# Weighted latent sums of sparse attention: 4-byte products replaced by three rounded ones

## Chip, cores and metric

The kernel runs on one core of a Trainium2 chip. The metric is the device time of one execution in microseconds (us); the median of a few runs is compared. The engines are TensorE (PE: matmuls, and transposes, which are matmuls against the identity), VectorE (DVE), ScalarE (ACT), GpSimd (POOL), and SyncE (SP), which issues the transfers. Each runs its own list of instructions in order, and they wait for each other by semaphores.

## What is computed

One decoder layer over 528 tokens (16 learned meta tokens and 512 others) of width 1024: a half-weighted SwiGLU layer, a mixer, a second SwiGLU layer, each followed by a residual sum and a layer norm. The change lies in the mixer's attention group (8 heads). An indexer scores every causal key, the 128 best of each query are kept, and all heads attend over one shared latent of 128 numbers per token:

```python
s = jnp.einsum('bqhc,bqkc->bqhk', q_lat, kv_sel) * (ATT_HEAD_DIM ** -0.5)
p = jax.nn.softmax(s, axis=-1)
o_lat = jnp.einsum('bqhk,bqkc->bqhc', p, kv_sel)          # the weighted latent sums
y_att = jnp.einsum('bthc,hcd->bthd', o_lat, w_uv)
```

The kernel keeps all keys and adds -1e30 to the scores of those not picked. The other head group, an mLSTM of 4 heads, is interleaved with attention.

## The kernel before

Tokens are cut into five tiles: tile 0 is the 16 meta tokens, tiles 1 to 4 have 128 tokens each. Most products are split products: ScalarE rounds a 4-byte operand to fp32r (`hi`), VectorE or GpSimd subtracts that from the operand (`lo`), and hi·hi + hi·lo + lo·hi is summed in PSUM (`split_product`). Each of the three is one TensorE instruction in the trace. Attention's products are plain 4-byte ones, and each is two instructions in the trace.

Attention works in 8 groups G of four heads: query tile j = 1 + G//2, heads 4·(G%2) to 4·(G%2)+3. Every engine has a loop over G = 0 to 8 written out by hand, and in step G it handles the scores of group G and the weighted sums of group G-1:

- **TensorE** (line 1733): `scores` (four, into two pairs of PSUM banks, so that score k waits for the masking of score k-2), `turn` (line 1696: transposes the four heads' exponentials of one key tile i into PSUM bank t%2, four instructions), `weigh` (line 1709: the latents of key tile i times the turned exponentials of four heads, 512 columns, summed over the key tiles 0 to j in bank 3). `project` (line 1717) and `turn_y` (line 1726) follow after every second group, and `turn_mlstm` brings in the other head group. For the last group, before the projections begin, there are five key tiles.
- **VectorE** (line 2377): `masked` (line 2331: score plus mask from PSUM into SBUF, with the row maximum, then its negative into nmax), `copy_even` (line 2363: turned exponentials of even t from PSUM to SBUF, which `weigh` reads), `normalise`, `att_lo` (the remainder of the attention output), the last rounds of the selection of tile 4 (`late_round`: maximum and replace, 8 keys each), `normed_mlstm` and `gated_mlstm` for the other heads.
- **ScalarE** (line 1098): `exps` (one exponential per head, with its row sum), `copy_odd` (line 1087), the copy of the finished sums into `olt`, `att_hi`, `mlstm_hi`, and one weight rounding (`hi`, line 725).

There are 28 turns and 28 weighs in all: 2, 2, 3, 3, 4, 4, 5, 5. In the order of before, step G of TensorE has the first two `scores`, `project` (of the pair finished in the step before), `turn` of tiles 0 and 1, the other two `scores`, then for each tile i the `turn` of tile i+1 (from the third on) followed by `weigh` of tile i, and at the end `turn_mlstm` and `turn_y`. On VectorE follow each other `masked` of the first two heads, `normalise`, `copy_even` of tiles 0 and 1, a late round, in step 2 the norm of the last mLSTM head (`normed_mlstm`), `masked` of the other two heads, the mLSTM gating, `copy_even` of the other tiles, `att_lo`, a late round.

Ahead of attention stand the mixer's projections (units 0 to 9), whose weights are rounded by ScalarE's `hi` and whose remainders are made by VectorE (`lo`) or GpSimd (`mix_lo`, line 627), and VectorE's selection (`select`, line 2194) and convolution (`convolve`, line 2231). GpSimd's list also has the causal masks (`causal_mask`, line 663), of which the last lets the `masked` of tile 4 begin.

## Time and profile before

| what | us |
|---|---|
| median of three runs (1017.17 to 1018.02) | 1017.67 |
| the profiled execution, its own time | 1017.49 |
| the span of its instructions | 1015.8 |
| around the span | 1.69 |

The profile is one execution, recorded by the hardware. Busy time is per engine; the end of a matmul is modelled, so a busy TensorE is not one at its peak. The chain of work is followed back from the last instruction, each step to what released it. In the chain a piece of TensorE is counted from completion to completion, so a row of it gives what an instruction adds when others stand next to it. The granted clock of TensorE was 1.00 of the higher of its two levels (2.4 GHz) in all the stretches shown below.

### The profile page before, as it was taken

The numbers are of one execution on the slowest core, as the hardware profiler recorded it, in microseconds if no ns is written. First come the engines' busy times: TensorE is split into PE (matmuls) and PEld (weight loads), VectorE is DVE, ScalarE is ACT, GpSimd is POOL, SyncE is SP. The second block draws the span as 40 slices with busy tenths as digits, with TensorE's granted clock in tenths as the row PEclk, the third lists the DMA queues.
The fourth block names the chain that finished last, engine by engine and source line by source line (L and its number), as shares of the span: only waits on it lengthen the run. The fifth ranks groups of instructions, "written<-read, shape, count | busy, mean of one in ns | idle before, by whom it ended". The sixth has DMA issues, their size and how long they took to land.

```text
span 1015.8 us, 18999 instructions
## 1 busy us (share of the span) xinstructions
PE 996.9 (98%) x7028; PEld 907.9 (89%) x7028; DVE 714.0 (70%) x1317; ACT 493.8 (49%) x868; POOL 118.1 (12%) x92
## 2 busy tenths in 40 slices
PE   9999999999999999999999999999999999999996
PEld 8999999999999988699765668889999999988886
DVE  6988888887322264699997523699989889942236
ACT  6656665566121264546346522576656665812121
POOL 0000000001121262045302205320000000000000
PEclk9999999999999999999999999999999999999999
DMA  7233332323223313132110102113323232333212
GB/s 252 84 100 107 102 105 90 116 80 105 86 86 111 113 44 116 36 123 82 44 42 1 43 1 83 43 42 126 124 83 124 85 121 96 125 103 101 98 57 84
DMA packets 30849, 90.48 MB, mean 89 GB/s; under 512 B 4689, under 2 KB 5329, under 8 KB 30801
## 3 DMA queue, kind: packets, MB, share of 16 engines
q1 hardware_dynamic: 30800, 89.83, 26.7%
q8 instruction: 31, 0.51, 0.2%
q14 instruction: 18, 0.14, 0.0%
HBM read 87.72 MB, written 2.10 MB: 88 GB/s over the span
## 4 chain that ended last, share of the span: by engine, by line
PE 81%; DVE 15%; ACT 2%; issue 1%; DMA 0%; SPq 0%; DVEq 0%; ACTq 0%
PE ps L1229 38%; PE ps L1287 22%; PE ps L1152 9%; DVE sc L2201 3%; DVE top L2200 3%; PE ps L1714 2%; PE ps L1424 1%; PE ps L1692 1%; DVE qk L2240 1%; PE ps L1705 1%; DVE wlo L1877 1%; PE ps L1489 1%; PE ps L1722 1%; PE ps L1337 1%; PE ps L1335 1%
## 5 line engine op out<-in xcount | busy, mean ns | idle before, releaser
L1229 PE MATMUL ps<-tsum,whi 128*128 128x264 f32 (+1 forms) x1280 | 243.1, 282 | 0.5 <-ACT ht L790 0.5
L1229 PEld LDWEIGHTS ps<-tsum,whi 128*128 128x128 f32 x1280 | 202.3, 188 | 0.7 <-issue 0.7
L1229 PE MATMUL ps<-tsum,wlo 128*128 128x264 f32 (+1 forms) x640 | 180.3, 282 | 0.0
L1229 PE MATMUL ps<-xh,whi 128*128 128x264 f32 (+1 forms) x480 | 135.4, 282 | 0.3 <-ACT sil L790 0.3
L1229 PE MATMUL ps<-xl,whi 128*128 128x264 f32 (+1 forms) x480 | 135.5, 282 | 0.0
L1229 PE MATMUL ps<-xh,wlo 128*128 128x264 f32 (+1 forms) x480 | 135.3, 282 | 0.0
L729 ACT ACTIVATE whi<-wraw 128x1408 fp32r<-128x1408 f32 (+1 forms) x48 | 74.6, 1555 | 123.0 <-PE ps L1287 123.0
L1787 DVE TENSOR_TENSOR wlo<-wraw,whi 128x1408 fp32r<-128x1408 f32 (+1 forms) x38 | 70.0, 1843 | 85.3 <-ACT whi L729 85.3
L1287 PE MATMUL ps<-hh,whi 128*128 128x264 f32 (+1 forms) x462 | 124.2, 323 | 0.0
L1287 PE MATMUL ps<-hh,wlo 128*128 128x264 f32 (+1 forms) x462 | 123.5, 322 | 0.0
L1287 PE MATMUL ps<-hl,whi 128*128 128x264 f32 (+1 forms) x462 | 123.4, 321 | 0.0
L777 ACT ACTIVATE whi<-ws 128x512 fp32r<-128x512 f32 x160 | 100.2, 628 | 42.5 <-PE ps L1229 40.5
L1229 PEld LDWEIGHTS ps<-tsum,wlo 128*128 128x128 f32 x640 | 120.2, 188 | 0.0
L1877 DVE TENSOR_TENSOR wlo<-ws,whi 128x512 fp32r<-128x512 f32 x160 | 109.5, 685 | 9.8 <-ACT whi L777 7.8
L1877 DVE TENSOR_TENSOR wlo<-wraw,whi 128x512 fp32r<-128x512 f32 x120 | 82.2, 686 | 26.2 <-ACT whi L777 26.2
L1152 PE MATMUL ps<-xh,whi 128*128 128x512 f32 (+1 forms) x296 | 96.2, 360 | 2.3 <-ACT xh L925 2.0
L1152 PE MATMUL ps<-xh,wlo 128*128 128x512 f32 (+1 forms) x296 | 92.6, 348 | 0.0
L1229 PEld LDWEIGHTS ps<-xl,whi 128*128 128x128 f32 x480 | 90.6, 189 | 0.0
L1229 PEld LDWEIGHTS ps<-xh,whi 128*128 128x128 f32 x480 | 90.1, 188 | 0.5 <-issue 0.5
L1229 PEld LDWEIGHTS ps<-xh,wlo 128*128 128x128 f32 x480 | 90.1, 188 | 0.0
L1152 PE MATMUL ps<-xl,whi 128*128 128x512 f32 (+1 forms) x296 | 88.0, 347 | 0.0
L777 ACT ACTIVATE whi<-wraw 128x512 fp32r<-128x512 f32 x120 | 74.7, 627 | 19.6 <-PE ps L1229 17.3
(287 smaller groups left out, 1828.0 us busy)
## 6 DMA issues: line engine op xcount, KB each, us to landing
wraw<-in_ffn_w_gate SPq DMA_DIRECT2D x43, 512.0 KB, 4.2
wraw<-in_ffn_w_up SPq DMA_DIRECT2D x42, 512.0 KB, 4.3
wraw<-in_ffn_w_down SPq DMA_DIRECT2D x32, 384.0 KB, 3.2
wraw<-in_ffn_w_down SPq DMA_DIRECT2D x32, 320.0 KB, 3.5
wraw<-in_w_in SPq DMA_DIRECT2D x19, 512.0 KB, 4.5
wraw<-in_w_out SPq DMA_DIRECT2D x8, 512.0 KB, 4.4
out<-zrow SPq DMA_DIRECT2D x8, 256.0 KB, 2.0
x<-in_x SPq DMA_DIRECT2D x3, 528.0 KB, 7.5
```

What stands on the lines that cost most here:

```text
L729: act.activation(whi[:, s, 0:width], wraw[:, s, 0:width], ACT.Copy).then_inc(w_hi, 1)
L777: act.activation(block_of(whi, b), block_source(g, b), ACT.Copy).then_inc(*done)
L1152: mm = pe.matmul(ps[:, b + e, 0:width], w, mov, start=(first and n == 0), stop=(last and n == 2))
L1229: mm = pe.matmul(ps[:, bank, 0:(HT, HALF_SEQ)[p // 2]], w[:, k * P:(k + 1) * P], v[:, k, :], start=(first and k == 0 and n == 0), stop=(k ...
L1287: mm = pe.matmul(ps[:, b + e, 0:width], w, mov, start=(kk == 0 and n == 0), stop=(kk == FT - 1 and n == 2))
L1335: pe.matmul(dst, w_h, a_h, start=(kk == 0), stop=False)
L1337: mm = pe.matmul(dst, w_h, a_l, start=False, stop=(kk == FT - 1))
L1714: pe.matmul(ps[:, 3, :], cmat[0:ROWS[i], i, :], pt_flat[0:ROWS[i], (t % 2) * 512:(t % 2 + 1) * 512], start=(i == 0), stop=(i == 1 + G // 2 ...
L1787: dve.tensor_tensor(wlo[:, s, 0:width], wraw[:, s, 0:width], whi[:, s, 0:width].bitcast(F32), ALU.subtract)\
L1877: dve.tensor_tensor(block_of(wlo, b), block_source(g, b), block_of(whi, b).bitcast(F32), ALU.subtract)\
L2200: link(dve.max(top8[:, r % 2, :], w))
L2201: link(dve.match_replace(w, top8[:, r % 2, :], w, TAKEN))
```

## The change

Each weigh becomes a split product. The latents are split once: ScalarE rounds them (`chi`, 128x640, on its list between the copies of `ct` and the rounding of unit 4's weights), GpSimd subtracts in place (`clo`) and builds `meta_c`, the rounded meta latents twice in 64 rows (`split_latents`, between `mix_lo(9)` and `causal_mask(3)`). Every turned tile is rounded by ScalarE (`weights_hi`) and its remainder is taken by VectorE (`weights_lo`), one after the other, in place of one copy by either; the three products are chi·hi, clo·hi and chi·lo. For the meta tile 32 rows are turned in place of 16, the remainder goes to rows 32 to 63 beside the rounded part, and two products do: clo on 16 rows and `meta_c` on 64.

The order of the three loops changes too. On ScalarE the roundings of tiles 0 and 1 stand ahead of the group's exponentials, those of tiles 2 to 4 between them. On VectorE the remainders of tiles 0 to 2 stand ahead of the third `masked`, that of tile 3 ahead of the fourth, that of tile 4 behind it; `normalise`, `att_lo`, the mLSTM work and the late rounds all stand behind the fourth `masked`. On TensorE `turn_y` moves one step later, behind the first two turns, and `project` also stands behind those turns. Two rounds of the late selection stand in step 4 and one in step 5, as before, but at the end of these steps.

```diff
-HEAD_GATED = ((1, 0), (1, 1), (2, 1), (3, 1))
-HEAD_HI = ((1, 1), (2, 0), (3, 0), (4, 0))
+HEAD_GATED = (1, 1, 2, 3)
+HEAD_HI = (2, 2, 3, 4)
-LATE_AT = ((4, 0), (4, 1), (5, 0))
+LATE_AT = (4, 4, 5)
...
+            c_parts = sb("c_parts", [P, NT, 256], F32R, s)
+            clo, chi = c_parts[:, :, 0:LAT], c_parts[:, :, LAT:2 * LAT]
...
+            pts = sb("pts", [P, NT * ML_H * VW], F32R, s)
+            meta_c = sb("meta_c", [64, LAT], F32R, s)
...
+        pt_h = [pts[:, e * 512:(e + 1) * 512] for e in range(2)]
+        pt_l = [pts[:, (2 + e) * 512:(3 + e) * 512] for e in range(2)]
...
+                def split_latents():
+                    pool.wait_ge(c_hi, 1)
+                    pool.wait_ge(ct_turned, 1)
+                    pool.tensor_tensor(clo, cmat, chi.bitcast(F32), ALU.subtract).then_inc(c_lo, 1)
+                    m = N_META
+                    link(pool.memset(meta_c[:, :].bitcast(F32), 0.0))
+                    for e, r in enumerate((0, 32)):
+                        pool.wait_ge(c_lo, e + 1)
+                        pool.tensor_copy(meta_c[r:r + m, :], chi[0:m, 0, :].bitcast(F32)).then_inc(c_lo, 1)
+                    pool.wait_ge(c_lo, 3)
...
                 mix_lo(9)
+                split_latents()
                 causal_mask(3)
...
                 act.activation(ct[:, END[3]:T], ps[:, 5, 0:P], ACT.Copy).then_inc(ct_ready, 1)
+                act.activation(chi[:, :, :], cmat, ACT.Copy).then_inc(c_hi, 1)
                 hi(MIX0 + 4, 0, UW, False)
...
+                def weights_hi(G, tiles):
                     for i in tiles:
                         t = TP0[G] + i
...
+                        R = META_ROWS if i == 0 else P
+                        act.wait_ge(pt_turned, t + 1)
+                        if t >= 2:
+                            act.wait_ge(pv_step, t - 1)
+                        act.activation(pt_h[t % 2][0:R, :], ps[0:R, t % 2, :], ACT.Copy).then_inc(pt_hi, 1)
+                late, turned_late = None, None
                 for G in range(GROUPS + 1):
...
+                    last_tile = 1 + (G - 1) // 2
+                    if G >= 1:
+                        weights_hi(G - 1, (0, 1))
+                    for q in range(4):
                         if G < GROUPS:
...
+                            exps(G, (q,))
+                        if G >= 1 and 2 + q <= last_tile:
+                            weights_hi(G - 1, (2 + q,))
+                    if turned_late is not None:
+                        att_hi(turned_late)
+                    turned_late = None
                     if G >= 1:
                         j, g = 1 + (G - 1) // 2, (G - 1) % 2
...
                         act.wait_ge(pv_step, TP0[G])
                         if G - 1 >= 2:
                             act.wait_ge(y_done, j - 1)
                         act.activation(olt[g], ps[:, 3, :], ACT.Copy).then_inc(ol_ready, 1)
+                        for h in range(ML_H):
+                            if HEAD_HI[h] == G:
+                                mlstm_hi(h)
                         if G == 4:
                             hi(MIX0 + 11, 1, UW, True)
...
+                        turned_late, late = late, j if g == 1 else None
...
+                        pe.wait_ge(pt_lo, t - 1)
                     for q in range(4):
...
+                        k0, k1 = (START[i], END[i]) if i else (0, META_ROWS)
+                        mm = pe.transpose(ps[0:k1 - k0, t % 2, q * P:(q + 1) * P], pbuf[G % 2][:, q, k0:k1], ident[:, :])
                     mm.then_inc(pt_turned, 1)
                 def weigh(G, i):
                     t = TP0[G] + i
...
+                    if i == 0:
+                        pe.wait_ge(pt_hi, t + 1)
+                        if G >= 1:
+                            pe.wait_ge(ol_ready, G)
+                        pe.wait_ge(c_lo, 3)
+                        m = N_META
+                        pe.matmul(ps[:, 3, :], clo[0:m, 0, :], pt_h[t % 2][0:m, :], start=True, stop=False)
+                        pe.wait_ge(pt_lo, t + 1)
+                        pe.matmul(ps[:, 3, :], meta_c[:, :], pt_h[t % 2][0:64, :], start=False, stop=False).then_inc(pv_step, 1)
+                        return
+                    pe.wait_ge(pt_hi, t + 1)
+                    pe.matmul(ps[:, 3, :], chi[:, i, :], pt_h[t % 2], start=False, stop=False)
+                    pe.matmul(ps[:, 3, :], clo[:, i, :], pt_h[t % 2], start=False, stop=False)
+                    pe.wait_ge(pt_lo, t + 1)
+                    pe.matmul(ps[:, 3, :], chi[:, i, :], pt_l[t % 2], start=False, stop=(i == 1 + G // 2)).then_inc(pv_step, 1)
...
+                late, turned_late = None, None
                 for G in range(GROUPS + 1):
                     last_tile = 1 + (G - 1) // 2
...
+                    if G < GROUPS:
+                        scores(4 * G)
+                        scores(4 * G + 1)
+                    if G == 0:
+                        turn_mlstm((0, 1))
                     if G >= 1:
...
+                        turn(G - 1, 0)
+                        turn(G - 1, 1)
+                    if late is not None:
+                        project(late)
+                    if turned_late is not None:
+                        turn_y(turned_late)
+                    if G < GROUPS:
+                        scores(4 * G + 2)
+                    if G >= 1:
+                        weigh(G - 1, 0)
+                        if last_tile >= 2:
+                            turn(G - 1, 2)
+                            weigh(G - 1, 1)
+                        if last_tile >= 3:
+                            turn(G - 1, 3)
+                    if G < GROUPS:
+                        scores(4 * G + 3)
+                    if G >= 1:
+                        for i in range(1 if last_tile < 2 else 2, last_tile + 1):
                             weigh(G - 1, i)
+                            if 4 <= i + 2 <= last_tile:
+                                turn(G - 1, i + 2)
                         if G in (1, 2):
                             turn_mlstm((G + 1,))
...
+                        turned_late, late = late, last_tile if (G - 1) % 2 else None
...
+                def weights_lo(G, tiles):
                     for i in tiles:
                         t = TP0[G] + i
...
+                        dve.wait_ge(pt_hi, t + 1)
+                        if i == 0:
+                            ins = dve.tensor_tensor(pt_h[t % 2][32:32 + META_ROWS, :], ps[0:META_ROWS, t % 2, :],
+                                                    pt_h[t % 2][0:META_ROWS, :].bitcast(F32), ALU.subtract)
+                        else:
+                            ins = dve.tensor_tensor(pt_l[t % 2], ps[:, t % 2, :], pt_h[t % 2].bitcast(F32), ALU.subtract)
+                        ins.then_inc(pt_lo, 1)
+                def late_rounds(G):
+                    for n, at in enumerate(LATE_AT):
+                        if at == G:
+                            select(4, LATE_ROUND + n, LATE_ROUND + n + 1)
+                turned_late = None
                 for G in range(GROUPS + 1):
                     last_tile = 1 + (G - 1) // 2
...
+                    if G < GROUPS:
+                        masked(4 * G)
+                        masked(4 * G + 1)
                     if G >= 1:
...
+                        weights_lo(G - 1, range(min(last_tile, 2) + 1))
+                    if G < GROUPS:
+                        masked(4 * G + 2)
+                    if G >= 1 and last_tile >= 3:
+                        weights_lo(G - 1, (3,))
+                    if G < GROUPS:
+                        masked(4 * G + 3)
+                    if G >= 1 and last_tile >= 4:
+                        weights_lo(G - 1, (4,))
+                    if late is not None:
+                        normalise(late)
+                    if turned_late is not None:
+                        att_lo(turned_late)
+                    if G in (0, 2):
+                        normed_mlstm((2 + G // 2,))
+                    for h in range(ML_H):
+                        if HEAD_GATED[h] == G:
+                            gated_mlstm((h,))
+                    late_rounds(G)
+                    if G >= 1:
+                        turned_late, late = late, last_tile if (G - 1) % 2 else None
```

## Rows read from the trace of the kernel before

**Rows 1.** The page: span, busy time of each engine, share and instructions.
```profile
span 1015.8 us, 18999 instructions
PE 996.9 (98%) x7028; PEld 907.9 (89%) x7028; DVE 714.0 (70%) x1317; ACT 493.8 (49%) x868; POOL 118.1 (12%) x92
```

**Rows 2.** Stretches of steps 2 to 8: start:end, length, busy us by engine, granted clock.
```profile
538.04:543.30 5.26, 5.26 (x26) 3.22 (x25) 4.54 (x18) 3.94 (x12) 2.54 (x2) 1.00 0.00 0
543.30:551.75 8.45, 8.45 (x47) 5.76 (x47) 5.07 (x17) 4.36 (x12) 1.27 (x1) 1.00 0.01 2
551.75:560.54 8.79, 7.30 (x27) 3.41 (x27) 6.87 (x20) 5.03 (x13) 1.27 (x1) 1.00 0.00 0
560.54:571.39 10.85, 10.65 (x54) 6.62 (x53) 6.61 (x20) 6.54 (x13) 4.36 (x2) 1.00 0.00 1
571.39:580.57 9.18, 9.18 (x41) 5.80 (x41) 5.21 (x15) 5.07 (x12) 1.39 (x3) 1.00 0.37 117
580.57:593.33 12.76, 12.76 (x69) 8.78 (x68) 6.22 (x17) 5.52 (x12) 0.00 (x0) 1.00 0.00 0
593.33:600.62 7.29, 6.97 (x31) 3.75 (x30) 2.09 (x4) 2.32 (x5) 0.00 (x0) 1.00 0.00 0
```

**Rows 3.** Chain of waits, steps 6 to 8 and behind: start, us, what.
```profile
571.39 1.78 PE ps L1692 x8
...
575.83 1.05 PE ps L1714 x2
576.88 0.59 PE ps L1705 x4
577.46 0.86 PE ps L1714 x2
578.32 0.44 PE ps L1705 x4
...
582.35 1.73 PE ps L1722 x16
...
600.62 2.80 PE ps L1152 x12
```

**Rows 4.** Groups by line and form, 527 to 610: count, busy us, mean ns, idle before.
```profile
L2370 DVE COPY v<-ps 128x512 f32<-128x512 f32 x8 | 5.5, 689 | 5.8 <-PE ps L1705 5.8
...
L2358 DVE TENSOR_TENSOR xl<-ps,xh 128x512 fp32r<-128x512 f32 x4 | 2.8, 691 | 11.0 <-ACT xh L1125 11.0
...
L1125 ACT ACTIVATE xh<-ps 128x512 fp32r<-128x512 f32 x4 | 2.4, 593 | 7.2 <-PE ps L1729 7.2
```

**Rows 5.** Timeline of VectorE in attention: start, us, line, operation.
```profile
532.80 1.10 DVE L2320 TENSOR_SCALAR upad<-upad,mv,mls 128x128 f32<-128x128 f32 x4
...
555.08 0.70 DVE L2200 MAX8 top<-sc 128x8 f32<-128x528 f32 x1
...
556.62 0.57 DVE L2340 CUSTOM_DVE_ANT_0 v<-ps,sc 128x400 f32<-128x400 f32 x1
...
566.44 0.43 DVE L2203 TENSOR_SCALAR sc<-sc 128x528 f32<-128x528 f32 x1
```

**Rows 6.** VectorE's waits for other engines, 428 to 531: total us, times, longest.
```profile
DVE wlo L1787 <- ACT whi L729: 0.3, 1, 0.3
```

**Rows 7.** One stretch of the projections, columns as in Rows 2.
```profile
431.30:473.00 41.70, 41.70 (x335) 40.19 (x334) 39.72 (x91) 23.10 (x34) 18.73 (x9) 1.00 0.31 102
```

**Rows 8.** Timeline of VectorE ahead of attention.
```profile
428.14 2.29 DVE L1787 TENSOR_TENSOR wlo<-wraw,whi 128x2048 fp32r<-128x2048 f32 x1 [0.31 <-ACT whi L729]
...
495.11 0.37 DVE L2203 TENSOR_SCALAR sc<-sc 128x400 f32<-128x400 f32 x1
```

**Rows 9.** One line of VectorE, the first convolution tap: shortest, median, longest ns.
```profile
L2238 DVE TENSOR_SCALAR qk<-upad,vec x4: 490/490/1672, 449.2 to 458.8; 128x528 f32<-128x528 f32 x4
```

**Rows 10.** Timeline of GpSimd.
```profile
445.96 4.61 POOL L630 TENSOR_TENSOR wlo<-wraw,whi 128x2048 fp32r<-128x2048 f32 x1 [2.51 <-ACT whi L729]
...
489.46 4.63 POOL L630 TENSOR_TENSOR wlo<-wraw,whi 128x2048 fp32r<-128x2048 f32 x1 [9.17 <-ACT whi L729]
495.62 0.29 POOL L666 TENSOR_SCALAR_AFFINE_SELECT sc<-sc 128x128 f32<-128x128 f32 x1 [1.53 <-DVE sc L2203]
```

More of the change, by code:

```diff
@@ L98 @@
 DROPS = END[1] - TOPK
+META_ROWS = 32
 def build(nc, a, out):
@@ L179, in build @@
             ct = sb("ct", [P, T], F32, s)
-            cs = sb("cs", [P, NT, 256], F32, s)
+            with ExitStack() as c_scope:
+                cs = sb("cs", [P, NT, 256], F32, c_scope)
+            c_parts = sb("c_parts", [P, NT, 256], F32R, s)
+            clo, chi = c_parts[:, :, 0:LAT], c_parts[:, :, LAT:2 * LAT]
             wuk = sb("wuk", [P, 4, LAT], F32, s)
@@ L184, in build @@
             upad = sb("upad", [P, 4 * (T + CONV - 1)], F32, s)
-            v1 = sb("v1", [P, NT, ML_H, VW], F32, s)
+            with ExitStack() as v_scope:
+                v1 = sb("v1", [P, NT, ML_H, VW], F32, v_scope)
+            pts = sb("pts", [P, NT * ML_H * VW], F32R, s)
+            meta_c = sb("meta_c", [64, LAT], F32R, s)
             sg = sb("sg", [P, 4, T], F32, s)
@@ L1710, in weigh @@
                     t = TP0[G] + i
-                    pe.wait_ge(pt_even if t % 2 == 0 else pt_odd, t // 2 + 1)
-                    if i == 0 and G >= 1:
-                        pe.wait_ge(ol_ready, G)
-                    pe.matmul(ps[:, 3, :], cmat[0:ROWS[i], i, :], pt_flat[0:ROWS[i], (t % 2) * 512:(t % 2 + 1) * 512],
-                              start=(i == 0), stop=(i == 1 + G // 2)).then_inc(pv_step, 1)
+                    if i == 0:
[13 more added lines that the diff above has]
+                    pe.matmul(ps[:, 3, :], chi[:, i, :], pt_l[t % 2], start=False, stop=(i == 1 + G // 2)).then_inc(pv_step, 1)
                 def project(j):
@@ L1730, in turn_y @@
                     mm.then_inc(yt_turned, 1)
-                late = None
+                late, turned_late = None, None
                 for G in range(GROUPS + 1):
                     last_tile = 1 + (G - 1) // 2
-                    for half in range(2):
-                        if G < GROUPS:
-                            for q in (2 * half, 2 * half + 1):
-                                scores(4 * G + q)
-                        if (G, half) == (0, 0):
-                            turn_mlstm((0, 1))
-                        if half == 0:
-                            if late is not None:
-                                project(late)
-                            if G >= 1:
-                                turn(G - 1, 0)
-                                turn(G - 1, 1)
-                    if G >= 1:
-                        for i in range(last_tile + 1):
-                            if 2 <= i + 1 <= last_tile:
-                                turn(G - 1, i + 1)
+                    if G < GROUPS:
[3 more added lines that the diff above has]
+                        turn_mlstm((0, 1))
+                    if G >= 1:
+                        turn(G - 1, 0)
[17 more added lines that the diff above has]
+                        for i in range(1 if last_tile < 2 else 2, last_tile + 1):
@@ L1751, in attention @@
                             weigh(G - 1, i)
+                            if 4 <= i + 2 <= last_tile:
+                                turn(G - 1, i + 2)
                         if G in (1, 2):
                             turn_mlstm((G + 1,))
-                        if late is not None:
-                            turn_y(late)
-                        late = last_tile if (G - 1) % 2 else None
+                        turned_late, late = late, last_tile if (G - 1) % 2 else None
                 pe.wait_ge(yml_lo, ML_H)
@@ L2377, in attention @@
+                        ins.then_inc(pt_lo, 1)
[4 more added lines that the diff above has]
+                turned_late = None
                 for G in range(GROUPS + 1):
                     last_tile = 1 + (G - 1) // 2
-                    for half in range(2):
-                        if G < GROUPS:
-                            for q in (2 * half, 2 * half + 1):
-                                masked(4 * G + q)
-                        if half == 0:
-                            if late is not None:
-                                normalise(late)
-                            if G >= 1:
-                                copy_even(G - 1, (0, 1))
-                            late_round(G, 0)
-                        if (G, half) in ((0, 1), (2, 0)):
-                            normed_mlstm((2 + G // 2,))
-                        if (G, half) in HEAD_GATED:
-                            gated_mlstm((HEAD_GATED.index((G, half)),))
@@ L2393, in attention @@
-                    if G >= 1:
-                        copy_even(G - 1, range(2, last_tile + 1))
-                        if late is not None:
-                            att_lo(late)
-                        late = last_tile if (G - 1) % 2 else None
-                    late_round(G, 1)
+                    if G < GROUPS:
+                        masked(4 * G)
+                        masked(4 * G + 1)
+                    if G >= 1:
+                        weights_lo(G - 1, range(min(last_tile, 2) + 1))
```

42 lines of the change are left out of this document (5 added, 37 removed).

## The prediction

> **What bounds the kernel now.** I read the page first: TensorE is busy in 98% of the span, VectorE in 70% [rows 1]. These are averages, so I went to the chain of waits and to the stretches. The chain runs over TensorE in the two SwiGLU layers, over VectorE's selection from 428 us on, and through attention from one engine to another. Attention's steps 2 to 8 take 62.6 us, in which TensorE is nearly always busy except in step 4, with 7.30 of 8.79 us [rows 2]. From the end of the weighed sums on TensorE runs projections without a pause, 0.233 us per 512-column product of rounded operands (2.80 us for 12) [rows 3]; what attention ends later or earlier, the kernel does too. So I look at two places: attention's steps, and the two splits of the latents ahead of it.
>
> **TensorE's own saving.** A weigh of a full tile adds 0.86 us now, that of the meta tile 1.05, and the transposes behind the latter 0.59 in place of 0.44 [rows 3]. Three rounded products are 3 x 0.233 = 0.70; I add 0.08 for the first one behind another kind of product (an estimate; the bounds are 0 and 0.19, the excess of the meta row): 0.78, so 0.08 saved. For the meta tile two products are 0.47, and each is loaded into another number of rows than the one before it. The rows price such a change at 1.05 - 0.86 = 0.19; with two, 0.85, so 0.20 saved. A change from 16 to 64 rows is in no row; its bounds are 0 and 0.19, and I take 0.19, the nearest row. In sum 20 x 0.08 + 8 x 0.20 = 3.2 us, where TensorE sets the pace. The Trainium skill (TensorEngine Tiling (Array Packing), Key Properties) says that another tiling mode, not just another tile, makes TensorE drain first, which speaks for the full price of both changes; if the one from 16 to 64 rows were free, the saving would be 1.5 us more.
>
> **What the saving costs elsewhere.** Before, one copy stood between turn and weigh, 0.69 us on VectorE or a shorter one on ScalarE; now a rounding of 0.59 on ScalarE and then a remainder of 0.69 on VectorE (the nearest forms, both from PSUM) [rows 4]. VectorE has 28 remainders for 14 copies, some 9 us more, and ScalarE 14 copies more. Both lists are in order, so a remainder that waits for its rounding holds the masked scores behind it. I laid the new lists out step by step with these durations and 0.04 us per handoff (an estimate), against the ends of the steps of before [rows 2]:
>
> - Step 1: two handoffs more, +0.3.
> - Step 2: the norm of the fourth mLSTM head (1.10 [rows 5]) moves from ahead of the third masked score to behind the fourth. TensorE's turn of that head now waits for it: +1.1.
> - Step 3: turn_y (0.44) leaves, two full tiles and the meta tile save 0.36; VectorE waits for the rounding of tile 2 with two masked scores behind it, but TensorE has project (1.73 [rows 3]) to do meanwhile: -1.0 with what it no longer waits.
> - Step 4: of before, 1.5 us were idle TensorE [rows 2], since a selection round (555.08 to 556.62, 1.54 us [rows 5]) stood between masked scores. Both rounds go behind them: -1.5, weighs -0.36, turn_y +0.44, small waits +0.1: -1.3.
> - Step 5: VectorE comes to its first masked score behind the two rounds. From the end of step 4's last exponential: att_hi 0.59, att_lo 0.69, rounds 3.08, masked score to its maximum 0.65, together 5.0 (4.85 with overlap). TensorE, from the same point: att_hi and the copy of the sums 1.2, project 1.9 with its latency, together 3.2, and then it wants the third score, which needs that maximum. It waits 1.6. Three smaller waits (last exponential, copy of the sums, first remainder) are 0.8; weighs -0.44, turn_y, which moves to step 6, -0.44: +1.5.
> - Step 6: the mask of tile 4 comes when the third round, now behind normalise, is done: normalise 0.8 (a product of the remainder's form, 0.69 [rows 4], and a small one), round 1.54, its closing 0.43 [rows 5], GpSimd's mask 0.3 [rows 10], masked score 0.8 (0.57 [rows 5] x 528/400, and its maximum): the third score can start 3.9 after step 5's last masked score. TensorE has there the last weigh, two scores (1.78), two turns and turn_y, 3.1. It waits 0.8, then 0.6 for the first remainder behind two masked scores; turn_y +0.44, old weighs -0.44, small waits -0.2: +1.2.
> - Step 7: TensorE sets the pace: turn_y -0.44, weighs -0.52, +0.2 for the last remainder: -0.8.
> - Step 8: no scores to fill in; each tile goes turn, rounding, remainder, weigh: +0.1.
>
> Sum: 0.3 + 1.1 - 1.0 - 1.3 + 1.5 + 1.2 - 0.8 + 0.1 = +1.1 us. What lies behind (projections, other weights) has slack: the last weight remainder on GpSimd moves some 8 us later, still far ahead of its use.
>
> **The splits ahead.** ScalarE's rounding of the latents (128x640; 0.59 for 512 columns [rows 4], so some 0.7) delays the rounding of unit 4's weights, and VectorE waits for that: 428.14 is its only wait for another engine until 531 [rows 6, 8]. Bounds: 0 and 0.7. I take 0. TensorE is busy all 41.70 us from 431.3, where unit 4's products begin, 0.9 after their remainders are there [rows 7, 8], so it and the engines that follow it are not moved. VectorE is, but at 449.2 its first convolution tap takes 1.67 in place of 0.49 [rows 9]: it ends at 450.87, just behind GpSimd's weight remainder, which ends at 450.57 [rows 10]. It was held 1.2 us by GpSimd, whose start came from TensorE; coming 0.7 later it is held 0.5.
>
> GpSimd's subtraction of the latents starts when its unit 9 is done, 494.09; at 4.63 us for 2048 columns [rows 10], 640 columns take some 1.5, to 495.6. VectorE comes at 495.11 with an instruction of the tap's kind [rows 8], and is held 0.5. Bounds: 0 (no clash), 1.5 (all of it). I take 0.5; nothing behind it waits for another engine before attention. The memory fill and two small copies follow beside other VectorE kinds: 0. The Trainium skill (SBUF — State Buffer, Who interferes with whom) says of VectorE's two-port forms and GpSimd that whichever comes first blocks the other for its whole instruction, which is what the tap's row shows; by it the price is 0.5, without it 0. It also says that VectorE with at most one operand in SBUF outside those forms does not clash, as the remainders have it.
>
> Total +1.1 + 0.5 = +1.6 us. The profiled execution took 1017.49 (span 1015.8 and 1.69 around it), 0.18 under the median; on the median's side I predict 1017.67 + 1.6 = **1019.3 us**. That is 0.16%, inside the 0.2% (2.0 us) which a measurement of this kernel can tell from no change.
>
> **Rivals.**
> 1. *Slower, through the longer handoff.* In steps 2 to 6 and 8 some 12 chains of turn, rounding, remainder and weigh follow each other with nothing to cover them (one in steps 2 and 3, two each in 4 to 6, four in 8). If each takes x more than my rows, the total is 1.6 + 12x: slower from x = 0.04 on; with x = 0.2 it is +4.0, 1021.7. For: each chain crosses three engines, and TensorE was idle 1.5 us in step 4 [rows 2] with a single copy in each. Against: the durations are those of the same forms. Chance 0.38.
> 2. *Faster: TensorE stays the bound.* If VectorE is ahead enough that the waits in steps 5 and 6 (1.6, 0.8 and 0.6) and in step 2 (1.1) do not form, the total is 1.6 - 4.1 = -2.5, or 1015.2; with the 3.2 us of cheaper weighs in full, less still, to 1014.4. For: TensorE was busy in all steps but one. Against: VectorE's list in steps 4 and 5 has two rounds ahead of the scores that TensorE wants. Chance 0.19.
> 3. *The rounded products are not what they seem:* if each of the three were two instructions as now, 0.86, the twenty full tiles alone would add 20 x 1.7 = 34 us, 1052. Against: products of the same types take 0.233 everywhere else. Chance 0.01.
>
> **How the numbers follow.** My forecast, no difference that can be told, has 0.42. Its terms with two-sided bounds: latents' rounding 0 to +0.7, GpSimd 0 to +1.5, tiling changes -1.5 to 0 (only half of it where TensorE sets the pace), handoffs about 1 us either way. The range reaches to the rivals: down to 1015.0 (waits not formed), up to 1022.3 (x = 0.25), and leaves 0.2 out, among it most of rival 2's lower half and the long handoffs. Faster by over 0.2% has 0.19, slower 0.39 (rivals 1 and 3).
>
> **What would show it.** In the changed profile, three rounded weigh products at about 0.23 each; VectorE's TENSOR_SCALAR at 495 lengthened to some 0.9, and its tap at 449 shortened by 0.7 with the same end; steps 2, 5 and 6 longer by 1.1 to 1.5 with TensorE waiting for VectorE at step 5's third score, and steps 3, 4 and 7 shorter by about 1. It is wrong if VectorE reaches attention over 1 us later than now, if steps 5 and 6 show no wait for the maxima, or if the handoffs of step 8 take over 0.5 us more than before.

## The result, and the profile after

The changed kernel takes 1020.32 us (median of 8 runs, 1020.12 to 1022.68), the kernel before beside it 1017.88 (8 runs, 1017.17 to 1018.38): a ratio of 1.003, interval 1.002 to 1.0039. That is +2.4 us where +1.6 was forecast: the time is inside the range, 1.0 us above the point, and the difference, 0.24%, lies just beyond the 0.2% that the prediction took as the limit of what can be told; its interval begins there. The profiled execution is the longest of the eight, 1022.68 us; 0.48 of that was there before the change is met at all (the same small activation of ScalarE starts at 422.17 us before and at 422.65 after).

The page of the changed kernel, span and busy times ([rows 1]):

```profile
span 1020.9 us, 19077 instructions
PE 998.6 (98%) x7048; PEld 914.9 (90%) x7048; DVE 724.2 (71%) x1331; ACT 500.8 (49%) x883; POOL 120.5 (12%) x96
```

Attention's steps 2 to 8 and then four finer stretches of the same view, columns as in [rows 2]; the third number from the end is the granted clock:

```profile
539.78:547.42 7.64, 6.57 (x27) 4.32 (x26) 5.37 (x19) 4.50 (x13) 0.01 (x1) 0.81 0.00 0
547.42:554.82 7.40, 7.40 (x46) 5.65 (x45) 3.75 (x13) 3.10 (x8) 2.49 (x2) 1.00 0.01 2
554.82:562.24 7.42, 7.14 (x34) 4.38 (x34) 6.10 (x19) 4.99 (x13) 1.28 (x1) 1.00 0.00 0
562.24:577.51 15.27, 13.22 (x52) 8.94 (x53) 10.98 (x29) 9.52 (x20) 1.28 (x1) 0.78 0.00 1
577.51:586.67 9.16, 8.98 (x49) 7.01 (x48) 7.21 (x19) 5.01 (x11) 5.79 (x4) 1.00 0.17 47
586.67:598.53 11.86, 11.86 (x69) 9.05 (x68) 7.88 (x21) 7.52 (x17) 0.00 (x0) 1.00 0.13 53
598.53:605.74 7.21, 7.08 (x39) 4.89 (x38) 4.28 (x8) 3.82 (x7) 0.00 (x0) 1.00 0.01 2
...
537.00:540.00 3.00, 2.28 (x11) 1.74 (x11) 2.38 (x9) 1.54 (x6) 0.00 (x0) 0.87 0.00 0
540.00:543.00 3.00, 3.00 (x13) 2.25 (x12) 1.21 (x6) 0.52 (x1) 0.00 (x0) 0.56 0.00 0
...
570.00:573.00 3.00, 2.81 (x8) 2.08 (x9) 1.13 (x3) 0.93 (x2) 0.00 (x0) 0.50 0.01 3
573.00:576.00 3.00, 3.00 (x9) 2.13 (x8) 2.19 (x6) 1.48 (x5) 0.00 (x0) 0.50 0.00 0
```

Step 3 became 1.05 us shorter, step 4 1.37, step 7 0.90 and step 8 0.08. Step 6 kept its length (9.16 for 9.18). Step 2 became 2.38 longer and step 5 4.42, and these two are the ones in which the clock is not 1.00, as it was in every row of attention before. The finer rows show where it fell, to about half (1.00 is 2.4 GHz, 0.50 is 1.2 GHz); the first fall begins in the end of step 1.

TensorE's timeline (start, us, line, operation, and in brackets the idle time ahead and what ended it) shows the new waits, and products of weighs of full tiles: two at the lower clock, then a whole weigh at the higher one:

```profile
538.93 0.85 PE L1701 MATMUL ps<-ident,upad 128*128 128x128 f32 x4 [0.72 <-DVE ht L2371]
...
546.77 0.66 PE L1701 MATMUL ps<-ident,upad 128*128 128x128 f32 x4 [1.07 <-DVE upad L2364]
...
568.55 0.94 PE L1717 MATMUL ps<-ct,ql 128*128 128x400 f32 x2 [1.53 <-DVE smax L2384]
...
572.25 0.63 PE L1748 MATMUL ps<-pts,c_parts 128*128 128x512 f32 x1
572.68 0.63 PE L1750 MATMUL ps<-pts,c_parts 128*128 128x512 f32 x1
...
583.02 0.48 PE L1747 MATMUL ps<-pts,c_parts 128*128 128x512 f32 x1
583.33 0.39 PE L1748 MATMUL ps<-pts,c_parts 128*128 128x512 f32 x1
583.56 0.39 PE L1750 MATMUL ps<-pts,c_parts 128*128 128x512 f32 x1
```

Products overlap, so the price is the distance between starts: 583.02, 583.33, 583.56, and the next kind at 583.79; at the lower clock 0.43 lies between two starts in place of 0.23. Both forecast waits are there, for the norm (546.77) and for the third score's maximum in step 5 (568.55).

Ahead of attention, VectorE and GpSimd near 495 us, answering to [rows 8, 10]:

```profile
494.56 1.57 POOL L691 TENSOR_TENSOR c_parts<-cs,c_parts 128x640 fp32r<-128x640 f32 x1
...
495.62 0.87 DVE L2247 TENSOR_SCALAR sc<-sc 128x400 f32<-128x400 f32 x1
```

### The profile page after: what moved, and what is told of

The parts are those of the page before. It is cut to its first block, busy times and chain, and to the rows that moved or that the text cites. A ratio compares the mean times of both kernels' runs of the same rounds, so it can differ in the third digit from the quotient of the medians.

```text
span 1020.9 us, 19077 instructions
## 1 busy us (share of the span) xinstructions
PE 998.6 (98%) x7048; PEld 914.9 (90%) x7048; DVE 724.2 (71%) x1331; ACT 500.8 (49%) x883; POOL 120.5 (12%) x96
## 4 chain that ended last, share of the span: by engine, by line
PE 80%; DVE 16%; ACT 2%; issue 1%; DMA 1%; SPq 0%; POOL 0%; DVEq 0%; ACTq 0%; POOLq 0%
PE ps L1254 38%; PE ps L1312 22%; PE ps L1177 9%; DVE sc L2245 3%; DVE top L2244 3%; PE ps L1449 1%; PE ps L1717 1%; PE ps L1731 1%; DVE qk L2284 1%; DVE wlo L1921 1%; PE ps L1514 1%; PE ps L1362 1%; PE ps L1360 1%; PE ps L1361 1%; DVE ql L2293 1%
```

## The experiments

The theory is the steps of the prediction: VectorE works its list in order, so that the norm and the maxima behind the late rounds come late, GpSimd's hold delays it further, and TensorE waits. A second part was added after the result was seen: the clock falls behind such waits and makes them dearer. The rival is the longer hand-off from ScalarE to VectorE. "Mean clock" below is the granted clock averaged over a whole execution.

**The norm ahead of step 2's maxima.**

```diff
+                    if G == 2:
+                        normed_mlstm((3,))
                     if G < GROUPS:
                         masked(4 * G)
...
-                    if G in (0, 2):
-                        normed_mlstm((2 + G // 2,))
+                    if G == 0:
+                        normed_mlstm((2,))
```

> The changed kernel, with the norm of the fourth mLSTM head moved on VectorE from behind step 2's masked scores to ahead of them, where VectorE waits 1.3 us for the first score. Theory (waits that the new order of VectorE's list makes, and a fall of TensorE's clock behind them): the 1.07 us wait of the turn of that head goes, step 2 is shorter by about 1.1 us, and if the lower clock around 540 us hangs on the waits of steps 1 and 2, it goes in part too; 1018.9 to 1019.3 us against 1020.3. Rival (the longer handoff per tile is the cost): step 3 waits for its roundings as long as before, later steps take up the gain, 1020.0 to 1020.4.

Measured: 1019.39 us (11 runs), ratio 1.0021 (1.0012 to 1.003), 0.9 less than the change. In its trace no wait for the norm is left in step 2. The time is just above the theory's 1018.9 to 1019.3 and below the rival's 1020.0; its interval overlaps that of the change, so the 0.9 is loose.

**One late round each in steps 3, 4 and 5**, and none in front of step 5's maxima.

```diff
-LATE_AT = (4, 4, 5)
+LATE_AT = (3, 4, 5)
...
-                        weights_lo(G - 1, range(min(last_tile, 2) + 1))
+                        weights_lo(G - 1, (0, 1))
+                        if G in (3, 5):
+                            late_rounds(G)
+                        if last_tile >= 2:
+                            weights_lo(G - 1, (2,))
...
+                    if G == 4:
+                        late_rounds(G)
                     if turned_late is not None:
                         att_lo(turned_late)
...
-                    late_rounds(G)
```

> The changed kernel, with the three late rounds of the selection where VectorE waits for a rounding or a copy: one ahead of the remainder of tile 2 in step 3, one between the last masked score and att_lo in step 4, one ahead of the remainder of tile 2 in step 5. Theory (waits of the new order, and the clock behind them): the 1.53 us wait of TensorE for step 5's third score goes, the mask of step 6 comes in time, TensorE's clock stays at its higher level from 570 to 577 us; 1.6 + 0.8 us of waits and up to 3 us of lower clock less: 1016.0 to 1018.0. Rival (handoff): the rounds only move, 1019.8 to 1020.5, and the clock falls as now.

Measured: 1016.67 us (11 runs, 1015.90 to 1019.37), ratio 0.9991 (0.9982 to 1.0): 3.65 less than the change, in the theory's range and clear of noise. In steps 5 and 6 the clock stayed up; its profiled execution, the longest, has a fall in step 2 (columns as above):

```profile
540.00:543.00 3.00, 2.79 (x10) 2.11 (x11) 1.37 (x6) 0.43 (x1) 0.00 (x0) 0.57 0.00 0
543.00:546.00 3.00, 3.00 (x15) 1.96 (x13) 2.10 (x6) 2.14 (x6) 0.00 (x0) 0.86 0.00 0
564.00:582.00 18.00, 17.26 (x93) 12.31 (x92) 14.57 (x40) 13.15 (x29) 7.07 (x5) 1.00 0.18 56
```

All the hand-offs are still in this kernel, so they are not what the change lost in step 5.

**GpSimd's split of the latents behind its last mask.**

```diff
-                split_latents()
                 causal_mask(3)
+                split_latents()
```

> The changed kernel, with GpSimd's split of the latents behind the causal mask of tile 3 in place of ahead of it. Theory: VectorE's TENSOR_SCALAR near 495 us takes 0.37 us again in place of 0.87, and all that follows comes 0.5 us sooner: 1019.8. Rival (that delay is taken up later, in waits of attention): 1020.3, no change.

Measured: 1021.23 us (6 runs, 1019.38 to 1021.94), ratio 1.0029 (1.0017 to 1.0041): no gain. The hold itself went, as VectorE's timeline shows:

```profile
495.54 0.37 DVE L2247 TENSOR_SCALAR sc<-sc 128x400 f32<-128x400 f32 x1
```

It starts 49.15 us behind GpSimd's weight remainder at the first convolution tap in both kernels (446.39 here, 446.47 in the changed one) and ends 0.5 sooner, and attention's first score follows 34.08 behind its end in both (529.99 and 530.57). Steps 5 and 6 together take 25.04 us in this execution against 24.43 in the changed kernel's, with a fall of the clock in step 5 of both; so the half us is seen at attention's start and not in the time, whose runs spread over 2.6 us. But this execution kept its clock up in step 2, and so gives that step's length without a fall:

```profile
538.99:545.30 6.31, 5.18 (x26) 3.43 (x26) 5.32 (x19) 4.39 (x13) 0.01 (x1) 1.00 0.00 0
```

**TensorE's wait in step 5 filled** with seven products whose result the first weigh overwrites.

```diff
...
+                    if G == 5:
+                        fill(7)
                     if G < GROUPS:
                         scores(4 * G + 2)
```

> The changed kernel, with seven additional products of rounded latents (512 columns, into the bank of the sums, which the next group's first product overwrites) on TensorE ahead of step 5's third score, where it waits 1.53 us. No wait is taken away. Theory (the clock falls because TensorE stood idle): the clock stays at its higher level behind step 5, the products cost nothing as the wait covers them, and the time is shorter by what the lower clock cost, 1 to 3 us: 1017.5 to 1019.3. Rival (the lower clock has nothing to do with that wait, or costs nothing since VectorE sets the pace there): no change, 1020.3, or more by what the products do not hide, up to 0.3.

Measured: 1019.93 us (11 runs), ratio 1.0017 (1.0008 to 1.0026): 0.4 less than the change, between theory and rival and not clear of noise. Steps 5 and 6 of its profile, at a clock of 1.00:

```profile
561.98:574.21 12.23, 11.71 (x60) 7.94 (x60) 9.50 (x26) 8.84 (x18) 1.28 (x1) 1.00 0.00 1
574.21:584.69 10.48, 9.16 (x49) 7.00 (x48) 8.51 (x22) 5.72 (x13) 5.75 (x4) 1.00 0.16 43
```

They take 22.71 us; in the changed kernel 15.27 + 9.16 = 24.43. So the fall behind step 5's wait cost that execution 1.7 us, after step 6 gave part of it back (VectorE went on meanwhile). The mean clocks bear on the rest: four of the 11 runs have 0.997, as most runs of the kernel before, and took 1018.45 to 1018.95; the other seven, at 0.995 or 0.996, took 1019.87 to 1020.54.

**All three moves together** (norm, rounds, GpSimd's split).

> The changed kernel with three moves at once: the norm of the fourth mLSTM head ahead of step 2's maxima, one late round each in steps 3, 4 and 5, and GpSimd's split of the latents behind its last mask. Theory (three separate costs: the 0.9 us measured for the norm, the 3.65 us for the rounds, the 0.5 us of GpSimd's hold at 495): 1016.7 - 0.9 - 0.5 = 1015.3 us, a granted clock of 1.00 throughout attention. Rival (the moves save the same time, each by letting TensorE run without a pause): 1016.2 to 1016.7 us.

Measured: 1014.29 us (6 runs, 1014.12 to 1015.61), ratio 0.9969 (0.9957 to 0.998), 6.0 less than the change and faster than the kernel before. In its profile the clock was 1.00 all through attention. It went 1 us below the theory, which added up medians that still held executions with a fall; whether that is the reason was not tested.

**A wait in the kernel before.**

```diff
+                def hold(n):
+                    v = sc[:, SC_OFF[4]:SC_OFF[4] + END[4]]
+                    for _ in range(n):
+                        link(dve.max(top8[:, 0, :], v))
...
+                    if G == 4:
+                        hold(9)
```

> The kernel before, whose products are untouched; only VectorE is given seven idle searches for maxima (about 0.73 us each) ahead of step 5's first masked score, so that TensorE waits there for the maxima and then for the meta tile's copy. Worked out from its trace the hold alone moves the meta tile's product in step 5 by about 2.5 us: 1020.2 us at a full clock. Theory (waits of about 1 us in this stretch bring the granted clock down, whatever the products): the clock falls to about 0.5 between 564 and 576 us, and the time is 1021.5 to 1023.1 us. Rival (the clock falls because of the change's products): clock 1.00 there and 1020.2 us or less.

Measured: 1026.31 us (5 runs), ratio 1.0081 (1.0068 to 1.0094). The expectation doesn't fit the kernel that ran: the searches stood a step too early (G == 4) and were nine. TensorE waited 6.45 us there, and the clock fell behind that:

```profile
555.00:558.00 3.00, 0.00 (x0) 0.00 (x0) 2.86 (x5) 0.00 (x0) 0.00 (x0) 0.91 0.00 0
558.00:561.00 3.00, 0.34 (x1) 0.34 (x2) 2.86 (x7) 0.17 (x1) 0.00 (x0) 0.50 0.00 0
```

A long wait does it with the products of before; whether short ones do was left to the next, with `hold(7)` at `G == 5`.

> The kernel before, its products and its order untouched; VectorE makes seven idle searches for maxima of tile 4 (0.73 us each, 5.1 us) ahead of step 5's first masked score, where it stood idle for 1.8 us. By the trace of the kernel before the third score then waits some 0.9 us for the first maximum and the meta tile's product another 1.1 us for its copy: 2.1 us at a full clock, 1019.5 us. Theory (such waits in attention bring the granted clock down, whatever the products): the clock falls to 0.5 to 0.9 between 560 and 575 us in the profile, and the median is 1020.8 to 1022.5 us. Rival (the clock falls because of the change's products): 1.00 there and 1019.5 us or less.

Measured: 1020.48 us (6 runs), ratio 1.0029 (1.0017 to 1.0041). The clock stayed at 1.00 through waits of 0.95, 0.67 and 1.04 us: +2.9 in place of 2.1, none of it by the clock (mean clocks 0.996 and 0.997 in all six). The theory on the clock missed, and the rival's 1019.5 was 1 us too low. With `hold(8)` the wait is as long as the changed kernel's:

> The kernel before with eight idle searches ahead of step 5's first masked score, one more than in the run with seven, so that TensorE's wait there is about 1.7 us (0.95 + 0.73), as long as the changed kernel's 1.53 us, with the products and the order of before. At a full clock: 1020.5 + 0.7 = 1021.2 us. Theory (one wait of this length is enough to bring the granted clock down, in most runs, whatever the products): the profile shows 0.5 to 0.9 between 563 and 576 us, the mean clock falls from 0.996 or 0.997 to 0.993 to 0.995, and the median is 1023 to 1025 us. Rival (the length of the wait alone doesn't decide): 1.00 there, mean clock 0.996 to 0.997 and 1021.2 us.

Measured: 1021.49 us (5 runs, 1020.97 to 1022.14), ratio 1.0035 (1.0021 to 1.0048), within 0.3 of the rival's number. Its wait in TensorE's timeline, and in the next fence the stretch around it:

```profile
566.70 1.68 PE L1692 MATMUL ps<-ct,ql 128*128 128x400 f32 x4 [1.70 <-DVE smax L2340]
```

```profile
561.00:576.00 15.00, 11.71 (x57) 7.12 (x56) 11.43 (x27) 7.25 (x14) 4.97 (x3) 1.00 0.01 2
```

TensorE idles 3.3 of 15 us and keeps its clock.

**The leading product alone**: two of the three products of a tile, VectorE's remainders and GpSimd's split are left out (of the edit, the products of a full tile are shown).

```diff
...
-                    pe.matmul(ps[:, 3, :], chi[:, i, :], pt_h[t % 2], start=False, stop=False)
-                    pe.matmul(ps[:, 3, :], clo[:, i, :], pt_h[t % 2], start=False, stop=False)
-                    pe.wait_ge(pt_lo, t + 1)
-                    pe.matmul(ps[:, 3, :], chi[:, i, :], pt_l[t % 2], start=False, stop=(i == 1 + G // 2)).then_inc(pv_step, 1)
+                    pe.matmul(ps[:, 3, :], chi[0:R, i, :], pt_h[t % 2][0:R, :], start=(i == 0), stop=(i == 1 + G // 2)).then_inc(pv_step, 1)
...
```

> The changed kernel with the leading product alone: it leaves out VectorE's remainders, GpSimd's split and two of the three products of every tile. Theory (VectorE's remainders are what makes TensorE wait): 20 x 2 x 0.23 + 8 x 0.43 = 12.6 us of products go, 3.7 us of waits and 0.5 us of GpSimd's hold; where TensorE then meets ScalarE's exponentials some of it is lost, so 1004 to 1010 us, and no wait for maxima at step 5's third score. Rival (the longer hand-off by ScalarE and its order make the waits): step 5's wait stays, and the time is over 1010 us.

Measured: 1008.59 us (4 runs), ratio 0.9913 (0.9899 to 0.9927). The time is in the theory's range, but its reason is not: step 5's wait is as long as with the remainders.

```profile
560.85 1.16 PE L1716 MATMUL ps<-ct,ql 128*128 128x400 f32 x2 [1.53 <-DVE smax L2373]
```

**The new order without the split.** From the kernel of the last experiment:

```diff
-                act.activation(chi[:, :, :], cmat, ACT.Copy).then_inc(c_hi, 1)
...
-                        act.activation(pt_h[t % 2][0:R, :], ps[0:R, t % 2, :], ACT.Copy).then_inc(pt_hi, 1)
+                        act.activation(pt_h[t % 2][0:R, :].bitcast(F32), ps[0:R, t % 2, :], ACT.Copy).then_inc(pt_hi, 1)
...
-                    pe.matmul(ps[:, 3, :], chi[0:R, i, :], pt_h[t % 2][0:R, :], start=(i == 0), stop=(i == 1 + G // 2)).then_inc(pv_step, 1)
+                    pe.matmul(ps[:, 3, :], cmat[0:R, i, :], pt_h[t % 2][0:R, :].bitcast(F32), start=(i == 0), stop=(i == 1 + G // 2)).then_inc(pv_step, 1)
```

> The new order of the queues without the split: ScalarE copies every tile unrounded, TensorE makes one product of it as before, and VectorE's remainders, ScalarE's rounding of the latents and GpSimd's split are gone; nothing of the result is left out. Theory (the remainders, not the order, are late in steps 2, 5 and 6): 1017.0 to 1018.4 us, clock 1.00 in attention. Rival (the order itself, with two late rounds at the end of step 4 and the norm behind the fourth masked score, makes the waits): 1019 us or more, with the wait for the maxima in step 5.

Measured: 1020.22 us (12 runs, 1017.68 to 1021.88), ratio 1.0027 (1.0018 to 1.0036): the rival. The order alone costs as much as the whole change. "Order" takes in one thing more: ScalarE makes all 28 copies, and the 14 that VectorE made before are gone from its list. Its profiled execution is the shortest, 1017.68 us, with the clock at 1.00 all through attention and the same wait:

```profile
564.99 0.94 PE L1715 MATMUL ps<-ct,ql 128*128 128x400 f32 x2 [1.53 <-DVE smax L2372]
```

So these waits form without the remainders, where the norm and the two rounds stand as in the change. Its 12 runs spread over 4.2 us, with mean clocks from 0.996 in the shortest to 0.993 or 0.994 in those over 1020.5: by that, one and the same kernel had falls of the clock in some executions and not in others; no trace shows where, since the profiled one has none. Then the moves of the first two diffs in this kernel:

> The new order with the norm and the late rounds moved as in the kernel with all three moves, but one product per tile as before, ScalarE's copies unrounded and no remainders; nothing of the result is left out. Against the kernel with all three moves it tells what the split itself is worth. Theory (the split saves TensorE the 3.2 us of the prediction): 1014.3 + 3.2 = 1017.5 us. Rival (the new order carries the gain: the order alone ran at 1017.7 us where the clock stayed up, with 0.9 us and 1.5 us of waits that the moves take out): 1015.3 us, so that the split is worth 1 us.

Measured: 1015.25 us (11 runs, 1014.89 to 1015.73), ratio 0.9977 (0.9968 to 0.9986), the rival's number. Its waits for the norm and for step 5's maxima are gone, which shows that their places in the list made them. Counted from attention's first transposes, its last weigh ends 2.4 us sooner than before (530.62 to 600.63; here 530.88 to 598.52), and 1.7 of that is there by the end of step 4 (560.55 and 559.10). Step 4's idle 1.5 us of [rows 2] are gone; by the profile, all that TensorE still waits for other engines in attention (total, times, longest) is:

```profile
PE ps L1699 <- DVE ht L2359: 0.5, 1, 0.5
PE ps L1729 <- ACT qi L1106: 0.3, 1, 0.3
PE ps L1715 <- DVE smax L2372: 0.2, 1, 0.2
```

With the split and all three moves the same view has these as well, 1.2 us of waits for remainders of weights (pts) and of the attention output (xl):

```profile
PE ps L1744 <- DVE pts L2412: 0.5, 2, 0.3
PE ps L1757 <- DVE xl L2402: 0.4, 1, 0.4
PE ps L1750 <- DVE pts L2415: 0.3, 1, 0.3
```

**The first mLSTM head's gate earlier**, on top of all three moves (and no longer behind step 1's work).

```diff
+                    if G == 1:
+                        gated_mlstm((0,))
                     if G < GROUPS:
                         masked(4 * G + 3)
...
-                    for h in range(ML_H):
+                    for h in range(1, ML_H):
```

> The kernel with all three moves, and the gate of the first mLSTM head ahead of step 1's fourth masked score, so that TensorE's turn of the third head in step 1 does not wait 0.7 us for it. Theory: up to 0.7 us less, 1013.6 us, and that wait gone from the profile. Rival (the fourth masked score, later by 0.7 us, is waited for in its place): 1014.3 us.

Measured: 1014.23 us (6 runs), ratio 0.9969 (0.9957 to 0.9981): nothing beside 1014.29, as the rival said. The wait fell from 0.72 to 0.26 us, and waits for the meta tile's remainder grew from 0.5 to 0.9.

## Why the prediction was right, and where it was not

The steps, each in us against [rows 2]. "Clock up" is the changed kernel's own step, but steps 1 and 2 from the execution with GpSimd's split later (step 2: 6.31 - 5.26) and steps 5 and 6 from the one with the wait filled (12.23 - 10.85, 10.48 - 9.18). Step 1 is counted from attention's first score: 529.54 to 538.04 before, 530.57 to 539.78 in the changed kernel, 529.99 to 538.99 with the split later.

| step | 1 | 2 | 3 | 4 | 5 | 6 | 7 | 8 | sum |
|---|---|---|---|---|---|---|---|---|---|
| predicted | +0.3 | +1.1 | -1.0 | -1.3 | +1.5 | +1.2 | -0.8 | +0.1 | +1.1 |
| measured | +0.71 | +2.38 | -1.05 | -1.37 | +4.42 | -0.02 | -0.90 | -0.08 | +4.09 |
| clock up | +0.50 | +1.05 | -1.05 | -1.37 | +1.38 | +1.30 | -0.90 | -0.08 | +0.83 |

- **Most of the lists were laid out rightly.** With the clock up every step is within 0.2 us of its term. The two waits forecast for steps 2 and 5 measured 1.07 and 1.53 us (1.1 and 1.6 predicted), and in step 6, with the wait of step 5 filled, TensorE waits 1.14 us for the late mask's score (0.8 predicted). The 3.1 us taken there for TensorE leave out the last weigh that the sentence names: two scores, two turns and turn_y make them up. They held, since that weigh was over when VectorE's last masked score of step 5 was (574.2 and 574.1).

```profile
578.44 1.16 PE L1717 MATMUL ps<-ct,ql 128*128 128x264 f32 x4 [1.14 <-DVE smax L2391]
```

- **In steps 1 and 4 the number was right by luck in part.** Step 1 has a 0.72 us wait for the gate of the first mLSTM head (538.93), which stands behind all of that step's VectorE work; the prediction gave that step only its hand-offs, and left out the 0.28 that by its own prices the weighs save there. In step 4 it put the 1.5 idle us of before down to a selection round (555.08 to 556.62). TensorE waited there for two of ScalarE's copies:

```profile
555.21 0.57 ACT L1094 ACTIVATE v<-ps 16x512 f32<-16x512 f32 x1
558.79 0.57 ACT L1094 ACTIVATE v<-ps 128x512 f32<-128x512 f32 x1
...
555.83 1.12 PE L1714 MATMUL ps<-v,cs 16*128 16x512 f32 x2 [0.48 <-ACT v L1094]
...
559.42 1.13 PE L1714 MATMUL ps<-v,cs 128*128 128x512 f32 x2 [1.01 <-ACT v L1094]
```

Each copy stood behind two exponentials. Those ahead of the first copy were over before the round could hold anything, so the 0.48 is not the round's; those ahead of the second waited for the scores behind the round. The change moved the round and also put ScalarE's roundings ahead of those exponentials, and no run has the one without the other, so what removed the 1.5 us is not shown.
- **TensorE's saving** was priced rightly: starts 0.31, 0.23 and 0.23 us apart make 0.77 for a full tile (0.78 predicted), and the meta tile's two products take 0.43 each, 0.86 (0.85 predicted; starts 591.93, 592.36 and the next kind at 592.79). The change from 16 to 64 rows, in no row of before, costs 0.20, the full 0.19 taken for it. The Trainium skill's rule (TensorEngine Tiling (Array Packing), Key Properties) agrees with that.
- **GpSimd's split** held VectorE's TENSOR_SCALAR for 0.5 us (0.87 against 0.37), as taken: it ends 0.4 behind GpSimd's subtraction (496.49 and 496.13), about its own length. Here the trace agrees with the Trainium skill's rule (SBUF — State Buffer, Who interferes with whom) too. VectorE's first masked score comes 1.02 us later than before (530.64 and 531.66), just past the 1 us that the prediction named as a sign of being wrong; 0.48 of it was there ahead of the change, and the 0.5 is this hold.
- **ScalarE's rounding of the latents** took 0.74 us and VectorE's wait grew from 0.31 to 0.94, at no cost: its tap ends 0.3 us behind GpSimd's weight remainder in either trace (450.87 and 450.57; 451.37 and 451.08). The sign by which that was to be seen, a tap shortened by 0.7, was wrong for this execution: the tap took 2.34, since VectorE had caught up in the gate's rows ahead of it (five small TENSOR_SCALARs of 2.15 us took 1.00); in the kernel with the wait filled it took 1.06 and again ended 0.3 behind.
- **What failed is "TensorE waits", as the cost of a wait in step 2 and step 5.** It was the wait alone; a clock below 1.00 stands nowhere in the sum. The clock that fell added 7.64 - 6.31 = 1.3 in step 2 and 1.7 in steps 5 and 6, some 3 us, to the profiled execution. The median has less of it: with 0.83 + 0.5 and no fall it would be 1017.88 + 1.33 = 1019.2 (an estimate), so some 1.1 us are left over, and they took the result from the likeliest case to the slow side of the 0.2%. That these are the clock's is argued. For it speak the four runs with the wait filled and a mean clock of 0.997 (1018.45 to 1018.95, some 1.2 above the kernel before beside them, 1017.67). Against it speak two runs of the changed kernel itself, which with a mean clock of 0.996 took 1020.12 and 1020.33, no less than three with 0.993 or 0.994 (1020.26 to 1020.31); only the remaining three, with 0.991 and 0.993, took longer.
- **Rival 1 (hand-offs)** would have shown in step 8, where four follow each other uncovered: -0.08, against the 0.5 more that was to prove it. **Rival 2 (TensorE stays the bound)** gave 1014.4 to 1015.2 for a kernel in which those waits do not form; that kernel, with the three moves, ran at 1014.29, GpSimd's 0.5 us among what they save. What was missing was its condition, that VectorE is ahead enough. **Rival 3** is out by the products' 0.23.
- **What the prediction did not separate is the split from the order.** The split against the same order without it is worth 1015.25 - 1014.29 = 1.0 us, out of 3.2 us of cheaper weighs; 1.2 us of new waits for remainders take part of the rest. The two intervals overlap, but all six runs of the last experiment's kernel (1014.07 to 1014.59) lie below all eleven without the split (1014.89 to 1015.73). The larger part of what there is to gain, 2.4 us, is the reordering, the 14 copies taken off VectorE with it, and above all what happens in step 4.

Three things stay open: what decides whether the clock falls, whether the median's 1.1 us are the clock's, and what removed step 4's idle time.

## What to carry to other kernels

When a change brings a new arithmetic and a new order of the queues, run the order alone: here it carried both the loss (two rounds ahead of the scores that TensorE wants, and a norm behind others) and most of the possible gain, and moving three pieces of work turned +0.3% into -0.3%. An in-order list on an engine that is not the bottleneck is priced by what stands in front of the one result that the busy engine waits for, not by its total. And give a new wait of TensorE an upper bound that holds a fall of the clock behind it.

## What the runs showed of the hardware

The clock of 1.00 that TensorE had in all of attention's rows fell to 0.50 to 0.57 for several us in some executions of the changed order. Ahead of a fall stood a wait of 0.72 us (step 1) or 1.53 us (step 5) within a stretch of other small waits; but the wait of 0.72 us in step 1 stood, with the clock at 1.00 behind it, in the profiles with the norm ahead, with the split later and with all three moves, and that of 1.53 us in the profile of the order alone. The product of 512 columns went from 0.39 to 0.63 us in the rows above when the clock fell. The new products alone do not seem to bring the fall (the order alone, with the old ones, has the spread of 4.2 us, and mean clocks down to 0.993). They are not ruled out as a part of it, since every fall that a trace here locates is in a kernel with rounded products, but the one behind 6.45 us. Nor does the length of the wait decide alone (1.70 us in the kernel before, the clock at 1.00 and 4 of 5 mean clocks at 0.996 or above); 6.45 us brought it. The Trainium skill (TensorE: Matmul & The Clock Gate, A second HAM failure mode: psum-queue depth-cycling) tells of a kernel in which short, frequent idle times make the clock swing between its levels; the changed kernel looks like it, but the 3.3 idle us of 15 in the kernel before, with no swing, say that frequent short waits are not enough.
